# Second-half expert routing split into two stages, expert jobs begun between them, and final sums moved to TensorE

## The reference

```
qh = (xb @ wq).reshape(blk, 8 heads, 2, 128)
s = einsum('thcd,hcnd->thcn', qh, keys)           # scores against 2 x 128 keys
sv, si = top_k(s, 16)                             # per half
cand = sv[:, :, 0, :, None] + sv[:, :, 1, None, :]
fv, fi = top_k(cand, 16)                          # 16 experts of each head
eidx = take_along_axis(cidx, fi);  g = softmax(fv)
act = gelu(einsum('thkd,td->thk', u[eidx], xb))   # "dots"
out = einsum('thk,thkd->td', g * act, v[eidx])    # "sums"
```

## Time and profile before

| | |
|---|---|
| median of 3 runs | 5932.22 us (5928.28 to 5935.11) |
| the profiled execution | 5921.76 us, span 5920.0 us |
| TensorE busy | 4190.6 us (71%) |
| VectorE busy | 3636.4 us (61%) |
| GpSimd busy | 2584.6 us (44%) |
| ScalarE busy | 1156.4 us (20%) |
| mean granted TensorE clock | 0.845 |
| moved by DMA | 1484.59 MB, mean 251 GB/s; the indirect gathers alone 1115.82 MB |

### The profile page before, as it was taken

One profiled execution on the slowest core, in us unless ns is written; L12 is line 12 of the kernel. 1 busy time (PEld: TensorE's weight loads), 2 busy tenths in 40 slices (PEclk: granted clock), 3 DMA queues, 4 the chain that ended last, 5 costly groups with the idle time before them and its releaser, 6 DMA issues. The chain is left out here.

```text
span 5920.0 us, 49064 instructions
## 1 busy us (share of the span) xinstructions
PE 4190.6 (71%) x15564; PEld 2567.8 (43%) x15564; DVE 3636.4 (61%) x7802; ACT 1156.4 (20%) x2892; POOL 2584.6 (44%) x2215
## 2 busy tenths in 40 slices
PE   6956981578677887379677777668677897265666
PEld 5334871443333665153335664453333675022222
DVE  4055528766677557576766768765668556845554
ACT  2042320111322111120422221111232211011011
POOL 0000010247555444336555443246545445477776
PEclk9975995788788998689888898879788998678788
DMA  4311740569777887579889975569777889599999
GB/s 131 115 56 54 243 132 0 178 238 322 253 256 257 315 286 269 193 271 381 304 276 328 387 260 167 188 213 338 252 258 258 281 306 311 217 343 349 347 357 342
DMA packets 579367, 1484.59 MB, mean 251 GB/s; under 512 B 60088, under 2 KB 251160, under 8 KB 572600
## 3 DMA queue, kind: packets, MB, share of 16 engines
q0 software_dynamic: 307200, 1115.82, 53.6%
q1 hardware_dynamic: 258952, 331.39, 16.8%
q10 hardware_dynamic: 12960, 34.26, 1.5%
HBM read 1435.37 MB, written 45.93 MB: 250 GB/s over the span
## 5 line engine op out<-in xcount | busy, mean ns | idle before, releaser
L2640 PE MATMUL duo<-vring,diag 128*128 128x512 f32 (+1 forms) x2544 | 1403.4, 697 | 626.4 <-DMA vring<-in_peer_v,eidx 365.7
L2526 POOL DMA_INDIRECT uring<-in_peer_u,eidx x1024 | 1248.8, 1219 | 1180.9 <-DVE uring L2558 707.6
L2593 POOL DMA_INDIRECT vring<-in_peer_v,eidx x1024 | 1158.3, 1131 | 1150.9 <-PE duo L2640 540.0
L2558 DVE SCALAR_TENSOR_TENSOR uring<-uring,xr 128x1024 f32<-128x1024 f32 x1040 | 1252.7, 1221 | 268.6 <-DMA uring<-in_peer_u,eidx 224.5
L2640 PEld LDWEIGHTS duo<-vring,diag 128*128 128x128 f32 (+1 forms) x2544 | 522.7, 219 | 1364.2 <-issue 1190.5
L2673 DVE SCALAR_TENSOR_TENSOR x_tok<-vring,wt,x_tok 128x1024 f32<-128x1024 f32 x404 | 522.1, 1292 | 379.0 <-DMA vring<-in_peer_v,eidx 352.5
L637 PE MATMUL duo<-wt,xT 128*128 128x512 f32 (+3 forms) x1440 | 607.5, 581 | 89.7 <-DMA wt<-in_w_in 89.7
L637 PEld LDWEIGHTS duo<-wt,xT 128*128 128x128 f32 (+1 forms) x1440 | 241.9, 179 | 444.8 <-issue 351.7
L2621 ACT ACTIVATE diag<-ident,wt 128x128 f32<-128x128 f32 x620 | 235.3, 397 | 1011.0 <-PE duo L2640 819.5
L492 PE MATMUL duo<-xT,wx 128*128 128x264 f32 (+1 forms) x1536 | 376.7, 409 | 37.9 <-DMA wx<-in_w_in 37.7
L492 PEld LDWEIGHTS duo<-xT,wx 128*128 128x128 f32 x1536 | 311.2, 205 | 92.8 <-DMA wx<-in_w_in 38.1
(11 more groups left out here) (462 smaller groups left out, 5076.1 us busy)
## 6 DMA issues: line engine op xcount, KB each, us to landing
wt<-in_w_in SPq DMA_DIRECT2D x32, 2048.0 KB
wx<-in_w_in SPq DMA_DIRECT2D x48, 1024.0 KB
wm<-in_w_in SPq DMA_DIRECT2D x32, 1024.0 KB
wm<-in_w_branch_a SPq DMA_DIRECT2D x32, 1024.0 KB
wq<-in_peer_wq SPq DMA_DIRECT2D x32, 1024.0 KB
tokm<-tout ACTq DMA_DIRECT2D x64, 256.0 KB
eb<-decays SPq DMA_DIRECT2D x32, 512.0 KB
s_h<-in_state_ssm SPq DMA_DIRECT2D x16, 1024.0 KB
```

The source lines that it names most:

```text
L2526: pool.indirect_dma_start(out=E.rings.urows[K % E.ur], out_offset=None, in_=table, in_offset=bass.IndirectOffsetOnAxis(ap=E.tiles[q][3][:, ...
L2558: dve.scalar_tensor_tensor(row, row, 1.0, G.xr[:, q % 2, :], ALU.mult, ALU.mult, accum_out=G.pre[:, q % 2, j:j + 1]).then_inc(G.dotted, 1)
L2593: pool.indirect_dma_start(out=E.rings.vrows[K % E.vr], out_offset=None, in_=table, in_offset=bass.IndirectOffsetOnAxis(ap=E.tiles[q][3][:, ...
L2640: mm = pe.matmul(G.bank[6 + c][0:m, :], G.diag[:, R % DR, 0:m], E.rings.vrows[K % E.vr][:, c * BANK:(c + 1) * BANK], start=first, stop=las ...
```

## The change

The stage "route" of a late half now routes its first tile and the sample tokens and deals these. Then the jobs of the half before are closed, the jobs of this half are begun, and a second stage, "route2", routes the second tile while the new U job runs beside it. The stages "early" and "lead" are gone. The last job's rings have 9 and 9 rows, in memory that is free at the end. `SHARES["last"]` is 0, so only 14 of the last 28 sums are VectorE's. The plans change a little: the first halves' V jobs do 7 and 50 sums in norm2 and pscore instead of 6 and 45, and 31 in route instead of 37.

```diff
-UR2, VR2 = 8, 7
+UR2, VR2 = 4, 5
...
     if H.late:
-        tiles.append((2, NS, 1, S.psl, S.es[:], S.gs[:]))
-    ends = (0.47, 0.94, 1.0) if H.late else (0.5, 1.0)
+        tiles = [tiles[0], (2, NS, 1, S.psl, S.es[:], S.gs[:])] if part == 0 else tiles[1:]
+    ends = (0.5, 1.0) if not H.late else ((0.9, 1.0) if part == 0 else (1.0,))
...
-        if H.late:
+        if H.late and part == 0:
             @block.sync
             def _(sp):
                 w = SLOTS // SREP
-                sp.wait_ge(sem("routed"), 3)
+                sp.wait_ge(sem("routed"), 2)
...
-                    peer_routes(nc, G, S, H, l, "route")
-                if (l, H.i) != (0, 0):
-                    G.beside.finish("U")
-                    G.beside.finish("V")
+                    peer_routes(nc, G, S, H, l, 0, "route")
+                    if (l, H.i) != (0, 0):
+                        G.beside.finish("U")
+                        G.beside.finish("V")
...
-                order = ("lead", "last") if last else ORDER[1 - H.i]
+                    order = ("route2", "last") if last else ORDER[1 - H.i]
...
-                if H.late and not last:
-                    with stage(nc, G, "early", "early") as (block, sem):
-                        pass
-        with stage(nc, G, "lead", "lead") as (block, sem):
-            pass
+                    if H.late:
+                        peer_routes(nc, G, S, H, l, 1, "route2")
...
-PLAN_DOTS = ({"early": 14, "vectors": 8, "norm1": 5, "xbc": 32, "tokproj": 90, "ssd": 10, "ssmout": 3, "attn0": 14, "attn1": 26, "mix": 54,
-              "lead": 32, "last": 237, "last_rush": 0.85},
+PLAN_DOTS = ({"route2": 22, "vectors": 6, "norm1": 5, "xbc": 32, "tokproj": 90, "ssd": 10, "ssmout": 3, "attn0": 14, "attn1": 26, "mix": 54,
+              "last": 247, "last_rush": 0.9},
...
-             {"ssd": 16, "ssmout": 6, "ssmst": 4, "qkv": 8, "attn0": 30, "attn1": 34, "mix": 40, "norm2": 6, "pscore": 45, "route": 37})
-SHARES = {"tokproj": 1.0, "ssd": 0.3, "attn0": 0.35, "attn1": 0.35, "mix": 0.8, "norm2": 0.5, "pscore": 1.0, "last": 0.25, "last_end": 0.5}
+             {"ssd": 16, "ssmout": 6, "ssmst": 4, "qkv": 8, "attn0": 30, "attn1": 34, "mix": 40, "norm2": 7, "pscore": 50, "route": 31})
+SHARES = {"tokproj": 1.0, "ssd": 0.3, "attn0": 0.35, "attn1": 0.35, "mix": 0.8, "norm2": 0.5, "pscore": 1.0, "last": 0.0, "last_end": 0.5}
```

More of the change, by code:

```diff
@@ L2387, in route_gates, with peer_routes @@
     own(dve.tensor_tensor(gates, e, B.den[0:n, 0:heads].unsqueeze(2).to_broadcast([n, heads, PK]), ALU.mult))
-def peer_routes(nc, G, S, H, l, key):
+def peer_routes(nc, G, S, H, l, part, key):
     NS = DECB * PH
@@ L2404, in _ @@
             own = Own(dve, sem("top"))
-            for j, n, heads, sc, rows, gates in tiles:
-                f0 = 0.0 if j == 0 else ends[j - 1]
-                fw = ends[j] - f0
+            for i, (j, n, heads, sc, rows, gates) in enumerate(tiles):
+                f0 = 0.0 if i == 0 else ends[i - 1]
+                fw = ends[i] - f0
                 for lo in range(0, 2 * heads, 4):
@@ L2422, in _ @@
                 go(f0 + fw * 0.97)
[L2423 removed]
+                dve.wait_ge(sem("pexp"), i + 1)
                 route_gates(dve, own, B, n, heads, gates)
                 dve.sem_inc(sem("routed"), 1)
[L2426 removed]
+                go(ends[i])
         @block.scalar
@@ L2430, in _ @@
             go = G.beside.by(act, "ACT")
[L2431 to L2434, removed]
+            for i, (j, n, heads, sc, rows, gates) in enumerate(tiles):
+                f0 = 0.0 if i == 0 else ends[i - 1]
+                go(f0 + (ends[i] - f0) * 0.96)
+                act.wait_ge(sem("centred"), i + 1)
                 act.activation(B.ef[0:n, 1, 0:heads], B.ef[0:n, 1, 0:heads], ACT.Exp).then_inc(sem("pexp"), 1)
-        if H.late:
+        if H.late and part == 0:
             @block.sync
@@ L2836, in hybrid_step @@
-                E = Experts(G, l, H, earlier, list(xr0), rings)
-                for q in range(len(E.tiles)):
-                    xr0[q % 2] += 1
-                order = ("lead", "last") if last else ORDER[1 - H.i]
-                dots, sums = PLAN_DOTS[1 - H.i], PLAN_SUMS[1 - H.i]
-                E.assign(spans(E, order, dots, sums), SHARES)
-                earlier = E.later()
-                G.beside.begin("U", Job(DOTS, E, E.dots_end, dots, order))
-                G.beside.begin("V", Job(SUMS, E, E.sums_end, sums, order))
@@ new lines, in hybrid_step @@
+                    E = Experts(G, l, H, earlier, list(xr0), rings)
+                    for q in range(len(E.tiles)):
+                        xr0[q % 2] += 1
+                    order = ("route2", "last") if last else ORDER[1 - H.i]
+                    dots, sums = PLAN_DOTS[1 - H.i], PLAN_SUMS[1 - H.i]
+                    E.assign(spans(E, order, dots, sums), SHARES)
+                    earlier = E.later()
+                    G.beside.begin("U", Job(DOTS, E, E.dots_end, dots, order))
+                    G.beside.begin("V", Job(SUMS, E, E.sums_end, sums, order))
```

16 lines of the change are left out of this document (14 added, 2 removed).

## The result

| | before | after |
|---|---|---|
| median | 5930.25 us (5915.26 to 5935.11, 4 runs) | 5861.43 us (5842.86 to 5876.68, 4 runs) |
| profiled execution | 5921.8 us | 5847.4 us, span 5845.7 us |
| last | 742.0 us | 673.7 us |
| TensorE, VectorE, GpSimd busy | 71%, 61%, 44% | 72%, 61%, 43% |

The ratio is 0.9887, with a 95% interval of 0.9846 to 0.9928. The change makes the kernel faster by 1.1%. I had predicted -14 us with a range down to 5872.0 us; it was -69 us by the medians and -74 us by the profiles.

What follows compares the result with a forecast made beforehand. GpSimd's gathers, lengthened beside VectorE's work, were taken to bound the last stage. Terms 21.2 - 20.2 - 3.8 - 2 - 9.5 summed to -14.3 us, 5917.9 us as a median, range 5872 to 5948 us.

Steps and rivals of the forecast that it cites:

- Term 1: Norm2 and pscore of both late halves: 1 + 5 more sums each, 1.83 us per pscore sum, +21.2 us together.
- Term 2: First routing stage: VectorE keeps 67.0 us, 31 TensorE sums fit beside it, waiting for ScalarE's Exp costs nothing.
- fourth rival: The split doesn't overlap: TensorE's sums outlast VectorE in the shortened route, each late half loses 34 us, 5986 us; chance 0.06.
- Term 3: Second routing stage: routing plus dots on VectorE, idle start time saved, -20.2 us in layer 1 and -3.8 us in layer 0.
- Term 4: Stages after layer 0's route2: 7.5 fewer dots left, helping only vectors and mix, -2 us (0 to -11).
- Term 5: Last: 10 more dots, less lengthening of gathers as sums leave VectorE, -9.5 us (bounds -101 and +15).
- The smaller rings: Last job's rings: cost nothing, since GpSimd waited only 12.6 + 0.3 us for free rows in 742 us.
- GpSimd set free: Last: without sums between them dots come singly, lengthening nearly vanishes, 5890 us, down to 5826 at DMA speed; chance 0.17.
- No relief: Last: dots alone lengthen the gathers as much as now, 757 us for the stage, 5942 us; chance 0.15.
- sums held up: Last: GpSimd stops before sums waiting for weights, delaying u gathers behind them, 6012 us or 5965 us; chance 0.12.
- The signs: Last near 732 us, mean gather about 1.12 us, GB/s near 360, TensorE share near 0.75; wrong if gathers under 1.05 us.

Runs made afterwards that it cites:

- e4: The changed kernel with the first halves' sums as before (6 in norm2, 45 in pscore, 37 in route): 5844.49 us, ratio 0.9879.
- e1: The changed kernel with last's quarter of sums given back to VectorE, each with a wait for its weights: 5848.9 us, ratio 0.9897.
- e3: The kernel before with only the last job's rings changed, to 9 and 9 rows: 5844.69 us, ratio 0.9888.
- e7: The kernel before with only the last job's VectorE sums made due three slots later: 5845.61 us, ratio 0.9878.
- f3: The kernel before with the last job's 24 ring rows dealt 12 and 12 instead of 13 and 11: 5828.13 us, ratio 0.9838.
- i2: The kernel before with rings of 12 and 12 rows and share 0 of VectorE sums in last, on the fourth chip: 5830.52 us, ratio 0.9854.
- e2: The kernel before with only last's VectorE share of sums set to 0, rings kept at 13 and 11 rows: 5839.29 us, ratio 0.9878.
- h2: The kernel before with rings of 12 and 12 rows and share 0 of VectorE sums in last, on the third chip: 5910.14 us, ratio 0.9957.

## Why the prediction was wrong

**What bounds last.** Right: GpSimd's issue of gathers, through their lengthening, and neither TensorE nor free rows. The views and the key quantity were the right ones.

**What the sums here can show.** Each kernel has one profile, and stages that no run changes differ between profiles: the mixer of layer 0's late half, all of it ahead of the first edit that acts, ends between 2168.7 and 2187.8 us in the 18 traces, at 2178.1 in before and 2171.6 in after. So only the length of a stage can be set against its term, not the time of its start.

**Term 1** (+21.2 us). From the end of the mixer's last matmuls to the start of route it took 5008.7 - 4878.5 = 130.2 us, before 4992.2 - 4876.4 = 115.8 us; in layer 0 129.4 and 116.5 us. Together that is +27.3 us. Pscore takes 108.7 us with 50 sums, 14.2 us more than before, where I had expected 9.1. A sum's price was not the 1.83 us midway between the two rows but 2.8 us. The DMA share there is 0.93, down from 0.98: 41 of the 50 sums waited for their row, 40.5 us in all.

**Term 2** (at 67.0 us). 67.8 and 67.2 us; 31 sums stand beside it, and the Exp isn't held up. The timeline of after:

```profile
5061.55 0.31 ACT L2435 ACTIVATE ef<-ef 128x128 f32<-128x128 f32 x1 [1.73 <-DVEq L2421]
...
5061.90 0.29 DVE L2385 TENSOR_REDUCE pden<-ef 128x8 f32<-128x128 f32 x1 [0.43 <-ACT ef L2435]
```

VectorE waits 0.43 us for it. The cover of 3 us held, and the fourth rival with it fell: TensorE's clock was 0.95 in the stretch. How thin the cover was, e4 shows: with six more sums the same wait is 9.08 us.

**Term 3** (-20.2 and -3.8 us). Route2 takes 84.4 us, 86.7 predicted, and its one idle gap before the first dot is 5.7 us, 5.3 predicted. From the start of route to that of last it is 5164.9 - 5008.7 = 156.2 us against 157.8: -21.8 us. In layer 0 it is 154.0 us, -6.4.

The two parts of routing by the earlier trace rows are 53.6 and 53.7 us long, not 53.4 as I had written, which is too little to matter here.

**Term 4** (-2 us) can't be read. What is left of the 5.3 us is -5.3 - 27.3 + 21.8 + 6.4 = -4.4 us; -6.5 of it arose ahead of the change (2178.1 and 2171.6 us), and +2.1 between the end of layer 0's stages and layer 1's late mixer, both within what unchanged stages differ by.

Terms 1 to 3 together: predicted -2.8 us, measured 27.3 - 21.8 - 6.4 = -0.9 us. That is near by luck: term 1 cost 6.1 us more than I had said, and term 3 gave 4.2 us more. Terms 1 to 4 agree even better, -4.8 predicted and -5.3 measured, and that is luck too.

**Term 5** (-9.5 us) is the step that failed: -68.3 us. Its parts were 618.3 us of undisturbed gathers, 97 us of lengthening, 19.2 us of rest, and -6 + 4 us: 732.5 us. In after GpSimd is busy 510.91 us with 499 gathers; at 0.94 us each that leaves 41.9 us of lengthening, and 673.7 - 618.3 - 41.9 = 13.5 us of rest. So 55 of the 59 us that I was too high are the lengthening. I had spread it evenly over VectorE's work ("sums are 91.3 of 369.4 us", hence 20% less of it). The runs show in its place that it doesn't go by the amount of work: e1 and e3 keep the sums and have 0.98 to 1.01 us per gather. It goes by where in a VectorE instruction a gather begins. In e1 even 196 of 308 gathers begin beside one, and those take 1.03 us on average; in before 134 of 269, and those take 1.43 us. The bunching that makes the difference comes with the 257 us of waits for v rows: without them (e7, f3) most of it is gone. I had these waits in hand, wrote that they starve GpSimd most, and priced them at -6 us, although the gathers of the earlier trace rows at 1.98 and 1.58 us stood beside the 0.94 of the earlier trace rows. Worked out from those, with all gathers at the pace of lead, the bound was -101 us; the measured value lies two thirds of the way there.

**The smaller rings** were costed at nothing since GpSimd hardly waited for a free row. That row answers whether a ring is too short. It says nothing of when a row is asked for: a gather's place in GpSimd's list hangs on the length of its ring (L2593 asks for row v + 11 at step v), and with the rings' difference the order of u and v gathers changes. e3 gives this edit alone -75.6 us by the medians.

**The rivals.** "GpSimd set free" (0.17) is what happened: it gave 5890 us, down to 5826 at DMA speed, and 5861 was measured. Its picture was right, dots come singly as rows land, and so was its evidence, lead. Its reason was not: "with no sums between them" isn't needed, as e1, e3, e7 and f3 keep them. Its objection, that a single dot still falls on every second gather, is worth little, since the gather begins before the dot or near its end: 1.00 to 1.06 us per gather. "No relief" (0.15) and "sums held up" (0.12) fell: no wait of GpSimd for weights is in after's last, and its waits for free v rows are 12.8 + 10.7 + 5.8 = 29.3 us, where 12.6 us stood before; none is longer than 0.3 us, the time of an issue, and the DMA engines are full beside them. What the second feared (a slow TensorE and GpSimd stopped behind it) was seen only on the third chip.

**The page's rule.** I had set the rule of the Trainium skill, "DMA: Bandwidth & Descriptors", section "Where 436 GB/s comes from", beside lead: about 358 GB/s as one core's share of HBM, so no 497 gathers under 728 us. Last took 673.7 us. It moved 389 GB/s over the whole stage, and i2 409 GB/s over 400 us. By the measurements that figure is no limit for one core running alone.

**The signs.** Of what I said would show it, two came out as warnings of exactly this: the mean gather under 1.05 us, and GB/s above the 360 expected. TensorE's share of last is 491.71 / 673.7 = 0.73, as expected.

## What to carry to other kernels

Where an engine takes work from two queues in a fixed order, look at what it waits for at the head of each, not at its busy share: a wait of a few us there can bring on a rush that slows another engine, and the next wait with it. Ring lengths do two things, they hold rows and they set when a row is asked for; vary their difference as well as their size. If a profile shows an operation at two durations (here 0.94 and 1.98 us), price the edit by both ends first, look at what runs when a long one begins, and ask which state the loop will settle in, rather than scale the mean. Before a difference of a few us between two profiles is explained, see how far stages that nobody changed lie apart in them.

## What the runs showed of the hardware

- The DMA engines gave one core 401 to 409 GB/s for 400 us of indirect gathers of 4 KB rows (after, e2, i2), as much as in 38 us of lead.
- In last, an indirect gather takes 0.94 us of GpSimd unless one of VectorE's two-input instructions on 128x1024 is running when it begins; then it ends 0.81 us after that instruction, about 2 us at most (262 of 269 gathers of before and all 307 of after within 0.06 us, 5300 to 5700 us). One that starts after the gather has begun costs it nothing (0.94 us, 5305.09 in after). Ahead of last the rule is looser, and gathers beside other instructions go up to 5.1 us (before).
- TensorE's mean granted clock in the middle of last (5300 to 5700 us) was 0.81 before with 395 matmul records, 0.86 in e3 with 448, and 1.00, which is the 2.4 GHz level, in after with 599.
- One program, h2 and i2, was 80 us apart on two chips, while the kernel before differed by 20 us between them. What on the chip, or at the time, makes it so isn't shown. A gain from filling the DMA engines can hang on it; a comparison with another version needs both on the same chip.
